# A weight ring of twenty slots over the mixer's buffers, and an experts' loop of five

## What is computed

```
h = rmsnorm(x);  proj = h @ w_in                 # w_in 1024 x 3584
x = x + concat(short_conv(...), hgrn2(...)) @ w_out      # recurrent states are outputs too
t = rmsnorm(x)
logits = t @ router_w + router_b;  top 4 of 32 experts, gates = softmax of the 4
for e in range(32):
    a = min(t @ w_gate[e] + b_gate[e], 7);  u = clip(t @ w_up[e] + b_up[e], -7, 7)
    hid = (u + 1) * a * sigmoid(1.702 * a)
    y += combine[:, e] * (hid @ w_down[e] + b_down[e])
out = rmsnorm(x + y) * final_norm_w
```

## Time and profile before

| | |
|---|---|
| median of 3 runs | 1135.92 us (1135.79 to 1138.27) |
| the profiled execution: its time, its span | 1137.09 us, 1135.3 us |
| PE busy | 1096.8 us, 97% |
| DVE, ACT, POOL busy | 394.7, 162.8, 23.2 us |
| DMA | 432.43 MB, mean 381 GB/s |

### The profile page before, as it was taken

The page is one execution under the profiler, slowest core; times in us unless marked ns, Lnnn a source line. Parts: engine busy times, 40 slices in busy tenths (PEclk is TensorE's granted clock), DMA queues, the critical chain, the costliest instruction groups (busy, mean ns, idle before and its releaser), DMA issues.

```text
span 1135.3 us, 15594 instructions
## 1 busy us (share of the span) xinstructions
PE 1096.8 (97%) x6308; PEld 448.9 (40%) x6308; DVE 394.7 (35%) x703; ACT 162.8 (14%) x284; POOL 23.2 (2%) x51
## 2 busy tenths in 40 slices
PE   8999999999999999999999999999999999999995
PEld 5656754433333333333333333333333333333332
DVE  4065375433333333333333333332333333223333
ACT  3101114211111111111111111111001110111112
POOL 0002000000000000000000000000000000000000
PEclk9999999999999999999999999999999999999998
DMA  9970345999999999999999999999999999999993
GB/s 315 334 230 20 130 159 221 353 427 426 436 430 429 430 430 434 433 429 434 431 429 434 431 433 432 429 435 429 431 434 427 426 431 428 429 428 428 428 427 135
DMA packets 39574, 432.43 MB, mean 381 GB/s; under 512 B 2991, under 2 KB 18163, under 8 KB 22261
## 3 DMA queue, kind: packets, MB, share of 16 engines
q1 hardware_dynamic: 37888, 428.13, 90.4%
q0 software_dynamic: 848, 3.03, 0.7%
q10 hardware_dynamic: 805, 0.82, 0.2%
HBM read 428.26 MB, written 3.71 MB: 380 GB/s over the span
## 4 chain that ended last, share of the span: by engine, by line
PE 69%; DMA 28%; DVE 1%; issue 0%; ACT 0%; SPq 0%; DVEq 0%
PE ps L1418 39%; DMA ring<-in_w_gate 22%; PE ps L1124 9%; DMA ring<-in_w_up 6%; PE ps L1391 4%; PE ps L1243 3%; PE ps L1308 3%; PE ps L1400 2%; PE ps L1311 1%; PE ps L1379 1%; PE ps L1461 1%; PE ps L1114 1%; PE ps L1373 1%; DMA consts<-in_consts 0%; PE ps L1152 0%
## 5 line engine op out<-in xcount | busy, mean ns | idle before, releaser
L1418 PE MATMUL ps<-ring,R 128*64 128x512 f32 x3072 | 691.1, 595 | 20.5 <-DMA ring<-in_w_gate 16.4
L1418 PEld LDWEIGHTS ps<-ring,R 128*64 128x64 f32 x3072 | 210.3, 137 | 421.7 <-issue 374.8
L973 DVE SCALAR_TENSOR_TENSOR x<-ps,gates,x 128x1024 f32<-128x1024 f32 (+1 forms) x93 | 102.8, 1106 | 135.4 <-PE ps L1391 132.1
L1124 PE MATMUL ps<-R,ring 128*128 128x320 f32 x384 | 107.5, 436 | 0.6 <-DVE R L686 0.6
L979 DVE TENSOR_TENSOR R<-ps,R 128x512 f32<-128x512 f32 x32 | 22.1, 691 | 228.9 <-ACT R L623 228.9
L1124 PEld LDWEIGHTS ps<-R,ring 128*128 128x128 f32 x384 | 71.8, 190 | 31.2 <-issue 1.8
L1391 PE MATMUL ps<-R 64*128 64x512 bf16 x558 | 76.8, 381 | 0.0
L1012 DVE TENSOR_SCALAR R<-ps 128x512 f32<-128x512 f32 x32 | 22.1, 691 | 146.6 <-PE ps L1418 146.6
L615 ACT ACTIVATE R<-R 128x512 f32<-128x512 f32 x32 | 20.2, 630 | 307.9 <-DVE R L1007 307.9
L1391 PEld LDWEIGHTS ps<-R 64*128 64x128 bf16 x558 | 20.8, 98 | 86.1 <-issue 51.9
L595 ACT ACTIVATE R<-ps 128x512 f32<-128x512 f32 x33 | 19.7, 597 | 240.3 <-PE ps L1311 240.3
(11 more groups left out here) (220 smaller groups left out, 565.8 us busy)
## 6 DMA issues: line engine op xcount, KB each, us to landing
ring<-in_w_gate SPq DMA_DIRECT2D x22, 4096.0 KB, 28.8
ring<-in_w_up SPq DMA_DIRECT2D x21, 4096.0 KB, 29.9
ring<-in_w_down SPq DMA_DIRECT2D x21, 4096.0 KB, 31.6
ring<-in_w_up SPq DMA_DIRECT2D x20, 2048.0 KB, 34.1
ring<-in_w_down SPq DMA_DIRECT2D x19, 2048.0 KB, 34.9
ring<-in_w_gate SPq DMA_DIRECT2D x18, 2048.0 KB, 32.7
ring<-in_w_in SPq DMA_DIRECT2D x14, 1024.0 KB, 13.1
ring<-in_w_down SPq DMA_DIRECT2D x6, 1024.0 KB, 12.7
```

The lines of the kernel that those rows point to most:

```text
L973: STT(xb[b], rows, gates[:, par, b:b + 1], xb[b], ALU.mult, ALU.add).then_inc(accDone, 1)
L1124: ins = MM(ps[:, n % 2, 0:NT], slot_k(L, 256)[:, k, 128 * half:128 * half + 128], hT[:, k, :], start=(k == 0), stop=(k == KT - 1))
L1418: ins = MM(shape(ps[64 * half:64 * half + 64, bank, :]), lhs(k), cols(w, half), start=False, stop=(k == KT - 1))
```

## The change

- **Ring.** `ring` gets 20 slots, five groups of four at slots 8, 12, 0, 4 and 16 (`GROUP_AT`); matrix i goes to group i mod 5. The fifth group, slots 16 to 19, lies over the mixer's `R3` (slots 16, 17 and a quarter of 18) and `R2` (the rest of 18, and 19), which are no buffers of their own any more. What the experts or the router's stage kept in `R2` and `R3` moves to a new buffer `RT` and to free parts of `R1`.
- **Temporaries** of an expert share five places: `hidT` lies over `ga`, `gt` over `gs`, `hid` over `gu`, `yrest` over `xgs`. For that ACT also waits for `yLow` ahead of its copy of gathered rows, and DVE waits for `hidTMM` ahead of the clip of the up product, no longer behind it.
- **Ahead of the experts** SP issues matrices 0 and 1 as before, then the write of the sample states (taken over from GpSimd), the first half of matrix 4 (when what lies in `R3` is used), matrix 2, and when `woutMM` is 3, matrix 3 and the second half of matrix 4.
- **Loads after that** are all written out, with no loop: matrices 5 to 11 and 84 to 95 in halves (95's second half in quarters), all others whole.
- **Router weights** are issued by SP behind those of `w_in`. **The final norm's weights** are no longer spread by DMA: they come with the small parameters (`parRows`, 60 rows for 52), and 16 small float32 matmuls spread them into banks 4, 5 and 2 of PSUM at the very end, ahead of the final scaling, which reads them there and waits for `fnwMM`.
- **Loops.** Experts 0 and 1 are written out, then a loop of six bodies of five experts; `PT`, `gates` and `eh` have three buffers, in the order 0, 1, 0, 1, 2.

The core of the diff:

```diff
+    GROUP_AT = (8, 12, 0, 4, 16)
+    NG_ = len(GROUP_AT)
+    SLOTS_IN_RING = 4 * NG_
+    FIRST = 2
+    PER_LOOP = NG_
+    LOOPS = (E - FIRST) // PER_LOOP
+    ML = 3 * PER_LOOP
+    HALVES_TO, HALVES_FROM = 12, MATS - 12
...
+        lastGroup = ring[:, GROUP_AT[-1]:GROUP_AT[-1] + 4, :].rearrange("p s n -> p (s n)")
+        R3 = lastGroup[:, 0:4608]
+        R2 = lastGroup[:, 5632:8192]
...
+        hidT, gt, hid, yrest = ga, gs, gu, xgs
...
+            for i in range(2):
+                for before in range(GROUP_AT[i], GROUP_AT[i] + 4):
+                    sp.wait_ge(projMM, load_done(before))
+                load_matrix(i, 0, i)
+            sp.wait_ge(stSOut, NH)
+            sp.dma_start(A["new_hgrn_sample"][0].rearrange("b h k v -> k (b h) v"), s0).then_inc(s0Out, 16)
+            sp.wait_ge(mixDone, NH)
+            sp.wait_ge(stSMM, 2)
+            sp.wait_ge(vSelDone, 2)
+            load_half(4, 1, 1, 0)
+            sp.wait_ge(s0Out, 16)
+            sp.wait_ge(biasDone, 1)
+            load_matrix(2, 0, 2)
+            sp.wait_ge(woutMM, 3)
+            load_matrix(3, 1, 0)
+            load_half(4, 1, 1, 1)
+
+            for i in range(NG_, MATS):
+                e, m = i // 3, i % 3
+                used = lambda n: 4 * (i - NG_) + n + START
+                if i < HALVES_TO or i >= HALVES_FROM:
+                    sp.wait_ge(wUsed, used(2))
+                    load_half(i, e, m, 0)
+                    if i == MATS - 1:
+                        sp.wait_ge(wUsed, used(3))
+                        load_quarter(i, e, m, 2, lateIn[i % NG_])
+                        sp.wait_ge(wUsed, used(4))
+                        load_quarter(i, e, m, 3, endIn)
                     else:
                         sp.wait_ge(wUsed, used(4))
-                        load_matrix(e, m, s)
-                        sp.sem_inc(lateIn[s // 4], 16)
-                if not ends:
+                        load_half(i, e, m, 1)
+                else:
+                    sp.wait_ge(wUsed, used(4))
+                    load_matrix(i, e, m)
...
-            pool.wait_ge(stSOut, NH)
-            pool.dma_start(A["new_hgrn_sample"][0].rearrange("b h k v -> k (b h) v"), s0).then_inc(s0Out, 16)
-
...
-            pool.wait_ge(woutMM, 3)
-            pool.dma_start(fnw[0], A["final_norm_w"].partition_broadcast(128)).then_inc(fnwIn, 16)
...
+                    act.wait_ge(yLow, scattered + START)
                     act.activation(xgs, ps[:, 3, :], ACT.Copy).then_inc(xgOut, 1)
...
                         dve.wait_ge(wUsed, e * LPE + 8 + START)
+                        dve.wait_ge(hidTMM, e + START)
                         TS(gu, ps[:, 1, :], LIMIT, -LIMIT, ALU.min, ALU.max).then_inc(uDone, 1)
                         dve.wait_ge(tDone, e + 1 + START)
                         dve.wait_ge(uDone, e + 1 + START)
-                        dve.wait_ge(hidTMM, e + START)
                         STT(hid, gu, 1.0, gt, ALU.add, ALU.mult).then_inc(hidDone, 1)
...
+            FN = 52
+            for k in range(D // 128):
+                row = ident[0:FN + 8, FN + k:FN + k + 1]
+                at = 128 * (k % 4)
+                MM(ps[:, 4 + k // 4, at:at + 128], row.broadcast_to([FN + 8, 128]), parRows[:], start=True, stop=True)
+                half = slice(64 * (k // 4), 64 * (k // 4) + 64)
+                ins = MM(ps[half, 2, at:at + 128], row.broadcast_to([FN + 8, 64]), parRows[:], start=True, stop=True)
+            ins.then_inc(fnwMM, 1)
```

More of the change, by code:

```diff
@@ L371, in _ @@
-            for n in range(BODIES - FINE, BODIES):
-                body(0, n, halves=True, ends=n == BODIES - 1)
             sp.wait_ge(roundsDone, 1)
             def all_loads(r):
-                with sp.Fori(0, BODIES) as it:
-                    body(r * (LPE * E), it)
+                for i in range(3 * FIRST):
+                    sp.wait_ge(wUsed, r * (LPE * E) + 4 * max(0, i - NG_ + 1) + START)
+                    load_matrix(i, i // 3, i % 3)
+                with sp.Fori(0, LOOPS) as it:
+                    for n in range(ML):
+                        i = 3 * FIRST + n
+                        sp.wait_ge(wUsed, r * (LPE * E) + it * (4 * ML) + (4 * (i - NG_ + 1) + START))
+                        load_matrix(i, it * PER_LOOP + i // 3, i % 3)
+                    sp.sem_inc(endIn, 16)
@@ L608, in one_round, with experts @@
                     bring_table(ACT.Sigmoid, 2)
-                with act.Fori(0, BODIES) as it:
-                    for j in range(PER_BODY):
-                        e = e0 + (it * PER_BODY + j)
-                        m = p0 + (it * PER_BODY + (j + 1))
+                def experts(it, these):
+                    for j in these:
+                        e = e0 + (it * PER_LOOP + j)
+                        m = p0 + (it * PER_LOOP + (j + 1))
                         act.wait_ge(aDone, e + 1 + START)
@@ L625, in one_round @@
                         act.activation(ysb[1], yrest, ACT.Copy).then_inc(yMid, 1)
+                experts(0, range(FIRST))
+                with act.Fori(0, LOOPS) as it:
+                    experts(it, range(FIRST, FIRST + PER_LOOP))
             one_round(0)
@@ L991, in one_round @@
                     weigh(0, 3)
[L992 removed]
+                keep_gates(p0, slice(0, 1), buf(0))
                 if isinstance(r, int):
```

245 lines of the change are left out of this document (103 added, 142 removed).

## The result

The changed kernel takes 1129.47 us (median of 4 runs, 1129.16 to 1129.89), the kernel before 1137.1 us beside it (4 runs, 1135.79 to 1138.66). The ratio is 0.9931, with an interval of 0.9916 to 0.9946: 7.6 us or 0.7% faster. The forecast was 11.7 us faster, 1124.2. The time lies inside the full range, 1121.8 to 1129.5, by 0.03 us, and outside the narrower one that the forecast gave for its own case, 1122.4 to 1127: the direction came out, and 4 us of the gain are missing. The profiled execution took 1129.68 us with a span of 1127.8, 7.5 under the span of before.

What follows compares the result with a forecast made beforehand. The prediction took the stream of weights to bound the experts. An earlier unbroken stream (-10.9 us) and fewer halves at the end (-0.8) gave -11.7, so 1124.2 us, with a range of 1121.8 to 1129.5.

Steps and rivals of the forecast that it cites:

- its own case: Whole kernel: the forecast 1124.2 us holds, with its own range of -13.5 to -9 us; chance 0.70.
- What bounds the kernel, and the lead as currency: Experts: the weight stream bounds them at 29.16 us each; PE needs 27.72 and eats its lead at 1.44 an expert.
- The main term: Extra ring group and load order from 199.7 us: matrix 12 lands at 295.9 for 306.8, -10.9 us (bounds -12.3, -7.3).
- Is a place always free in time, ahead of the experts: Ring places free at least 2 us early, no charge; states and matrix 2 through before 199.7, cost 0, at worst 1.5.
- the cited rule: DMA queues ahead of the experts: engines alternate between queues with work, serve one in order; states land at nearly the old time.
- The end of the stream: Last matrices: 12 in halves instead of 24, 0.07 us saved on each of 12, -0.8 us; PE catches up without loss.
- The experts' own work: Expert loop: two new waits, on ACT and DVE, are for events over 10 us old; shared temporaries cost 0.
- The tail: Behind the last scatter: 16 small matmuls take 3.3 us, hidden before the final scaling with 0.35 to spare; 0, up to +1.
- a sign of being wrong: End of the kernel: the forecast is wrong if, among other signs, the final scaling waits for the small matmuls.
- half the gain: Stream not unbroken at 214 or 293, or states and matrix 2 late at 199.7: -8 to -4 us, 1128 to 1132; chance 0.16.

Runs made afterwards that it cites:

- the two kernels with a smaller lead: Changed kernel, matrix 4's halves both behind matrix 3: span 1134.5 us; kernel with grouped small matmuls, both also after matrix 0's first quarter is read: span 1131.9 us.

## Why the forecast was right, and where it was not

**What bounds the kernel, and the lead as currency: right.** The gain of the first 300 us stood at 1094.58, and the two kernels with a smaller lead were still behind by what they had lost, within 0.6 us. PE ran free for eight experts longer (540.90 to 763.49); the forecast said about six, though its own 11.7 us at 1.44 an expert make eight. It also set PE's first wait at 570.05, where a first one of 0.39 us came an expert earlier.

**The main term: right in sum, and partly for another reason.** Matrix 12 was forecast at 295.9 and landed at 296.1. Counted from the issue of matrix 3 it came 107.1 us later before and 97.0 after, -10.1; forecast -10.9. The other 0.7 us of the difference at the end is that the mixer of this execution ended earlier. The working named the loads of the final norm as one cause, by the 2.6 us that matrix 3 gained on landing. That part is worth 0.7 us by itself; matrix 3's landing counts only because the place for half of matrix 4 was there as well.

**Is a place always free in time, ahead of the experts: right.** Matrix 2 was issued when the states had landed, the copy on ACT ended at 174.9 (forecast 175.5), and matrix 2 was through at 194.1, 5 us before it mattered. The states took their turn behind matrix 1, which landed at 173.6, and were through 6.0 us later; served in order, as the cited rule has it, and at 179.6 not far from the 177.6 of before. The working had the write beside matrix 1 in the kernel before; there its packets began only at about 168 us and moved 0.2 of their 2.1 MB before 172, so the new order had little sharing to end. No row shows a stall of the stream on PE between 217 and 296.

**The end of the stream: right as far as it can be measured.** From matrix 12's landing to the last half of `w_up` the stream took 799.3 before (906.39 - 107.1) and 798.5 after: -0.8. The run with 24 halves gave +0.65 back.

**The experts' own work: right.** PE's two new waits are in no row of the chain, and an expert takes 27.7 where PE is free.

**The tail: the step that failed.** It said that sixteen small matmuls take 1.95 + 1.32 = 3.3 us and end 0.35 us before they are needed, so 0, and up to +1. Measured: +4.0, and the final scaling waited for the small matmuls, which the forecast had named as a sign of being wrong. The count and the two prices were fair: in groups they take 3.63 us. But the rows they came from are runs of one tile shape each, and the new code alternates two shapes (and banks), which costs 0.16 us a change; it then ran into the lower clock. A margin of 0.35 us was taken as cover for a term that came out 4.1 us longer, and the cap of +1 had no row behind it. The second part, the later additions, wasn't foreseen at all: VectorE's branch was in the code before, where 0.8 us were lost behind it, and nothing in the working asks what it would cost in the new program.

Of the rivals, half the gain named 1128 to 1132, and 1129.5 lies in it, but for a reason of its own: its mechanism, a stream with gaps, did not happen. That the time stayed inside the full range is therefore luck: its upper end was set for that rival, and nothing in it stood for a tail 4 us longer. The sum by steps: -0.66 (mixer) - 10.09 - 0.77 + 4.02 = -7.5 in the span, as measured.

The version to use is the changed kernel with the small matmuls in two groups, 1126.53 us: 10.8 us less than before beside it (1137.33), and about 3 less than the change as it was made.

## What to carry to other kernels

Where a stream of loads is the bound, a lead at its start is still there at the end (here 5.2 us at matrix 12 and 5.4 at the end), but only where the next places are free in time: without that 0.7 of 2.3 us were left in one kernel and 0.35 of 4.9 in another. So look for one more free place at its start, and follow each landing until the stream is unbroken. Price matmuls by a row in which the same shapes follow each other in the same order, and sort them by tile shape when they don't depend on each other. The last few microseconds, where nothing overlaps any more, want as much care as the large term: a margin of 0.35 us under an estimate of 3.3 is no cover.

## What the runs showed of the hardware

- Matmuls of float32 with 60 rows, 128 columns of weights and 128 moving: 0.26 us each in a row, with 64 columns 0.20; alternating, a pair takes 0.77 instead of 0.45.
- The granted clock fell to 0.50 at about 1117.8 in the changed kernel, while PE was shown busy with small matmuls from 1113.18 on (the last float32 product had ended at about 1109); the same small matmuls then took 1.33 us a pair instead of 0.77. In another execution of such a tail it fell 2.5 us behind the first small matmul instead of 4.6.
- Behind a branch over code that isn't executed VectorE stood still for 2.5 us, shown as issue in the profile, with two packets in an instruction queue; without the branch the gap was 0.5 us. In another program the same two packets came with no such gap.
- A single core drew 426 to 434 GB/s in every slice of 28.2 us from 226 to 1100 us; single matrices in it took up to 11.3 us and not 9.7.
